# Attention visits in two half steps, five PSUM banks for scores and two for projections, in a two-block forward pass

## The chip, the cores and the metric

The kernel is one program on one core of a Trainium2 chip. A core has TensorE (matmuls, written into PSUM), VectorE, ScalarE and GpSimd (elementwise work) and SyncE, which issues most of the DMAs here. Each runs its own list of instructions in order, and they wait for one another on semaphores. PSUM has eight banks of 128 x 512 fp32. The metric is the device time of one launch in microseconds; several runs are made and the median is compared.

## The reference

Two model blocks follow one another on x of 512 tokens by 1024 channels in fp32. The first block, in which the change lies, is:

```python
h = rms_norm(x, norm_gain, RMS_EPS)
(qa, ka, va, ga, qb, kb, vb, gb, qc, kc, vc, fc, gc, gm) = split(h @ w_in)
ya = diff_attention(qa, ka, va, lam, slopes_a)           # A: 4 heads, each two softmaxes over 64 channels, p0 - lam*p1
ya = rms_norm(ya, subln_gain, SUBLN_EPS) * (1 - lam_init)
yb = sliding_window_attention(qb, kb, vb, sinks, slopes_b)  # B: 8 heads, window of 128
yc = forgetting_attention(qc, kc, vc, log_sigmoid(fc + b_forget))  # C: 8 heads, decay by a cumulative sum
ua, ub, uc = (ya*silu(ga)) @ w_up_a, (yb*silu(gb)) @ w_up_b, (yc*silu(gc)) @ w_up_c
gates = sigmoid(gm)                                      # three gates of 1024
x = x + (gates0*ua + gates1*ub + gates2*uc) @ w_o
```

The attentions are causal over blocks of 128 queries. The second block (a gated recurrence, a linear attention, a short convolution, a convolutional FFN of 2816 channels, an embedding gate) comes afterwards and is not changed.

## The kernel before

**Tiles.** Activations lie with channels on the partitions and the 512 tokens on the free axis. A projection tile is 128 output channels by 512 tokens, one PSUM bank, summed over eight blocks k of 128 input channels. Each k takes three matmuls, for both operands are split into a high part in the fp32r format and the rest: high by high (L911), high by low (L912), low by high (L914). So a tile is 24 matmuls of 128x512. Weights come in units of four blocks (half a tile): SyncE loads a unit into `raw`, ScalarE makes `whi` (L1247), GpSimd makes `wlo = raw - whi` (L2191). There are 5 `raw` and 6 `whi` and `wlo` buffers; a unit is split five units ahead of its use (`LOOK`), and the load of unit u+5 waits on SyncE until `wlo` of unit u is done.

**The order of the work.** `Plan` writes one list of steps, and every engine's program follows that list in order (`follow`), taking from each step what is its own. A step placed between two others therefore stands between them in every engine's queue. `take(ring, tile)` gives a tile a bank, the one of its ring that was taken longest ago, and TensorE waits (`free`) until the bank's last holder has been read. The ring "S" is for scores, transposes and small sums; its banks are 4, 5, 6 and bank 3 as well while projections use "first3" (0, 1, 2). During the value projection vA, which needs four banks at once ("main", 0 to 3), "S" is 4, 5, 6.

**Attention visits.** Attention runs between projection tiles. `pipeline(groups)` is a generator that yields after each visit; `step` advances it, and `slot(i)`, called after each k of a projection tile, calls `step` after k = 7. vA calls it after every second k. Each attention has 16 groups (C and B: a pair of heads for one query block; A: one head for one query block, with two softmaxes). A visit takes two groups, i and i+1. Groups 4t, 4t+1 have keys 128 and 256 wide and 4t+2, 4t+3 have 384 and 512 (B: never over 256). A visit's steps are, in this order:

1. `normal` of group i-1: VectorE divides the exponentials of the second group of the visit before by their sum;
2. `take` of four banks, then `pair` or `scores`: TensorE computes scores (L1016 for B and C, L1030 for A); VectorE adds the bias, finds the maximum and writes P (L1774), which empties the bank; ScalarE takes the exponential in place with its sum (L1322). For C, VectorE builds the bias first from rows N and a column;
3. `pre` for the next visit: SyncE fetches rows N of a head (L2305, C), VectorE makes a head's bias (A, B);
4. `values` of groups i-4, i-3: TensorE multiplies the transposed P by V (L1065); after a head's last block VectorE copies y, and for A ScalarE squares it;
5. `turn` of groups i-2, i-1: TensorE transposes P (L1041) into a bank of "S", ScalarE copies it to SBUF (L1334). It needs `normal` of that group. C has four such tiles where the groups are wide (their width doesn't fit two to a bank), else two;
6. `normal` of group i;
7. for A, every second visit, `late`: TensorE sums the squares (L1071), ScalarE forms the norm (with loads of a table), VectorE applies it.

P has six buffers; P of a group is written again by the score six further on.

**The projections around it.** Ahead of the first visit are kA0 and kA1; then kA and qA tiles run under C's visits, vA too; kB, vBt, qB under A's; the four gateC tiles under A's last ones; nine `gm` tiles under A's last and B's visits; gateA, gateB afterwards. After a tile its `out`, `gate_out` or `gm_out` copies it out of its bank (ScalarE L1310, L1306, L1373; for qB, kB and the gates VectorE as well). In each queue that step stands behind the visit that was called after the tile's k = 7, and ahead of step 1 of the next visit.

Of the kernel before, what the change touches and what calls it, by code (L numbers as in the profile page):

```python
# [132 lines left out]
class Plan:  # L133
# [21 lines left out]
    def add(self, *step):  # L155
        self.steps.append(step)

    def take(self, ring, tile):
        banks = {"main": (0, 1, 2, 3), "first3": (0, 1, 2), "S": (), "Y": (7,), "m3": (0, 1, 2), "x5": (3, 4, 5, 6, 7),
                 "x4": (3, 4), "all": (0, 1, 2, 3, 4, 5, 6, 7)}[ring]  # L160
        if ring == "S":
            banks = self.score_banks
        if ring in ("S", "main", "first3"):
            self.hold(min(banks, key=lambda b: self.held.get(b, -1)), tile)
            return
        n = self.turn.get(ring, 0)
        self.turn[ring] = n + 1
        self.hold(banks[n % len(banks)], tile)
# [29 lines left out]
        self.advance(self.background)  # L198

    def slot(self, i):  # L200
        if i == 7:
            self.step()

    @staticmethod
# [14 lines left out]

    def pipeline(self, groups):  # L220

        n, kind = len(groups), groups[0][0][0]
        for g in groups[0:2]:
            for u in g:
                self.add("pre", *u)
        for i in range(0, n + 6, 2):
            two = groups[i:i + 2]
            if 0 < i <= n:
                for u in groups[i - 1]:
                    self.add("normal", *u)  # L230
            for g in two:
                for u in g:
                    for m in range(2 if kind == "A" else 1):
                        self.take("S", ("scores", *u, m))
                if kind != "A":
                    self.add("pair", *g)
                for u in g:
                    self.add("scores", *u)
            for g in groups[i + 2:i + 4]:
                for u in g:  # L240
                    self.add("pre", *u)
            for g in groups[i - 4:i - 2] if i >= 4 else ():
                _, h, j = g[-1]
                y = ("y" + kind, h if kind == "A" else h // 2 if kind == "C" else h % 4)
                if j == 0:
                    self.take("Y", y)
                self.add("values", kind, h, j)
                if j == 3 and kind != "A":
                    self.ready.add(y)
            for g in groups[i - 2:i] if i >= 2 else ():  # L250
                self.turns(g)
            if two:
                for u in two[0]:
                    self.add("normal", *u)
            if kind == "A" and i >= 6 and groups[i - 5][0][2] == 3:
                h = groups[i - 5][0][1]
                self.take("S", ("late", h))
                self.add("late", h)
                self.ready.add(("yA", h))
            yield  # L260

    def turns(self, units):

        kind, _, j = units[0]
        wd = P * (min(j, 1) + 1) if kind == "B" else P * (j + 1)
        together = [units] if len(units) * wd <= T else [[u] for u in units]
        for us in together:
            slot = self.slots % (4 if kind == "C" else 3)
            self.slots += 1
            for n, u in enumerate(us):  # L270
                self.slot_of[u] = slot, n * wd
            self.slot_before[us[0]] = self.slot_user.get(slot)
            self.slot_user[slot] = us[-1]
            self.take("S", ("turn", *us[0]))
            self.add("turn", *us)

    def stages(self):
        add, take = self.add, self.take
        self.ready = set()
        add("begin")  # L280
        for k in range(KD):
            add("first", k)
            if k <= LOOK:
                self.split_to(k)
        add("lambda")
        for m in range(4):
            take("main", ("kC", m))
        for k in range(KD):
            self.enter("win", k, KC)
            add("kC", k)  # L290
        take("S", ("norm1",))
        add("norm1")
        for m in range(4):
            add("kC_out", m)
        self.tile("S", ("qC", 0))
        take("S", ("columns1",))
        add("columns1")
        add("out", "qC", 0)
        self.tile("S", ("qC", 1))
        add("out", "qC", 1)  # L300
        for m in range(4):
            take("main", ("vC", m))
        take("Y", ("vF", 0))
        for m in range(1, 4):
            take("S", ("vF", m))
        for k in range(KD):
            self.enter("win", k, VC)
            add("vC", k)
            add("x_norm", k)
        add("fc")  # L310
        for half in range(2):
            for m in range(4):
                add("vC_out", half, m)

        def sums(i):
            if i == 5:
                take("S", ("sums",))
                add("sums")

        self.tile("main", ("qC", 2), between=sums)  # L320
        add("out", "qC", 2)
        self.tile("main", ("qC", 3))
        add("out", "qC", 3)
        take("S", ("cq",))
        add("cq")
        c, a, b = softmax_units()
        self.background.append(self.pipeline(c))
        add("masks")
        self.score_banks = (4, 5, 6, 3)
        for name in ("kA", "qA"):  # L330
            for t in range(4):
                self.tile("first3", (name, t), between=None if (name, t) == ("kA", 0) else self.slot)
                add("out", name, t)
        self.score_banks = (4, 5, 6)
        for m in range(4):
            take("main", ("vA", m))
        for k in range(KD):
            self.enter("win", k, VA)
            add("vA", k)
            if k % 2:  # L340
                self.step()
        for m in range(4):
            add("vA_out", m)
        self.background.append(self.pipeline(a))
        self.score_banks = (4, 5, 6, 3)
        for name in ("kB", "vBt"):
            self.tile("first3", (name, 0), between=self.slot)
            add("out", name, 0)
        for t in range(4):
            self.tile("first3", ("qB", t), between=self.slot)  # L350
            add("out", "qB", t)
            if t == 0:
                take("S", ("vB",))
                add("vB")
        self.background.append(self.pipeline(b))

        def gate(name, y, t):
            while (y, t) not in self.ready:
                self.step()
            self.tile("first3", (name, t), between=self.slot)  # L360
            add("gate_out", name, t)

        def gm(d, j):
            take("first3" if self.background else "main", ("gm", d, j))
            self.proj(("gm", d, j), "win", GM + 1024 * j + P * d, between=self.slot)
            add("gm_out", d, j)

        for t in range(4):
            gate("gateC", "yC", t)
        add("masks_in")  # L370
        for d in range(3):
            for j in range(3):
                gm(d, j)
        for t in range(4):
            gate("gateA", "yA", t)
        for t in range(4):
            gate("gateB", "yB", t)
        while self.background:
            self.step()
        add("rg_const")  # L380
        for d in range(8):
            if d >= 3:
                for j in range(3):
                    gm(d, j)
            for n in "cab":
                take("main", ("up", n, d))
                self.proj(("up", n, d), "up_" + n, P * d, range(4))
                add("up_out", n, d)
            add("merged", d)
        add("x_again")  # L390
        for d in range(2):
            take("main", ("wo", d))
            self.proj(("wo", d), "wo", P * d, range(7), stop=False)
        for d in range(8):
            if d < 2:
                self.proj(("wo", d), "wo", P * d, [7], start=False)
            else:
                take("main", ("wo", d))
                self.proj(("wo", d), "wo", P * d)
            add("wo_out", d)  # L400
        self.second(add, take)
# [2045 lines left out]
```

## Time and profile before

| | us |
|---|---|
| median of 3 runs | 1276.0 (1275.64, 1276.0, 1281.35) |
| the profiled execution | 1279.9 |
| its span in the profile | 1278.1 |
| TensorE busy | 1234.3 (97%) |
| VectorE busy | 658.9 (52%) |
| ScalarE busy | 550.4 (43%) |
| GpSimd busy | 659.0 (52%) |
| TensorE's mean granted clock | 0.987 |

The profile comes from one execution. Its span runs from the first instruction to the last; the execution took 1.8 us more. PE is TensorE's matmuls, PEld its weight loads (they overlap the matmuls), DVE VectorE, ACT ScalarE, POOL GpSimd, SP SyncE. Matmuls are pipelined: two of 128x512 start 0.23 us apart although each row shows one as 0.39 long. PEclk is the clock that TensorE was granted as a share of full speed: 1.00 is 2.4 GHz and 0.50 is 1.2 GHz.

### The profile page before, as it was taken

The page shows a single profiled execution, that of the slowest core. Times are in us where ns is not written, and L with a number is a line of the kernel's source. Part 1 is how long each engine was busy: PE and PEld are TensorE (multiplying, and loading weights), DVE is VectorE, ACT ScalarE, POOL GpSimd, SP SyncE. Part 2 cuts the span into 40 slices and gives each one's busy share as a digit, 9 for nine tenths or more (in the row PEclk, how much of TensorE's full clock was granted, in tenths as well). Part 3 has the DMA queues.
Part 4 walks back from the last instruction along what each step waited for, and adds up shares of the span by engine and source line. Part 5 has one row for each costly group of instructions (what it writes and reads, how often), then busy time and mean ns, then how long its engine had stood idle before and what let it go on. Part 6 is the DMA issues. An engine that isn't in the chain of part 4 may idle for free.

```text
span 1278.1 us, 17097 instructions
## 1 busy us (share of the span) xinstructions
PE 1234.3 (97%) x6230; PEld 982.5 (77%) x6230; DVE 658.9 (52%) x1217; ACT 550.4 (43%) x1066; POOL 659.0 (52%) x501
## 2 busy tenths in 40 slices
PE   7998989999999999999989999999999999999996
PEld 5886767777878888888776676878888888888885
DVE  6436744765743312125277545459999999200024
ACT  4544544676654333235552647542332333322344
POOL 4772223235346544446454464646767776655542
PEclk9998999999999999999988999999999999999998
DMA  5333222113222433343231121423333333433321
GB/s 197 112 113 98 67 61 73 50 50 83 67 66 83 114 92 91 95 152 112 82 84 50 42 71 53 116 82 84 99 99 99 90 92 87 128 96 94 100 74 66
DMA packets 63939, 113.94 MB, mean 89 GB/s; under 512 B 7016, under 2 KB 12776, under 8 KB 63856
## 3 DMA queue, kind: packets, MB, share of 16 engines
q1 hardware_dynamic: 63712, 112.84, 31.0%
q8 instruction: 50, 0.82, 0.3%
q14 instruction: 33, 0.27, 0.1%
q10 hardware_dynamic: 144, 0.00, 0.0%
HBM read 110.71 MB, written 2.11 MB: 88 GB/s over the span
## 4 chain that ended last, share of the span: by engine, by line
PE 83%; DVE 9%; ACT 3%; issue 2%; POOL 1%; DMA 1%; DVEq 0%; SPq 0%; ACTq 0%; POOLq 0%
PE pb L911 24%; PE pb L912 24%; PE pb L914 24%; PE pb L1065 2%; PE pb L1041 1%; DVE P L1774 1%; PE pb L1016 1%; POOL HL L2191 1%; DVE B L1644 1%; PE pb L979 1%; DVE U L1644 1%; DVE sq L1632 1%; PE pb L981 1%; PE pb L980 1%; POOL wlo L2191 1%
## 5 line engine op out<-in xcount | busy, mean ns | idle before, releaser
L2191 POOL TENSOR_TENSOR wlo<-raw,whi 128x512 fp32r<-128x512 f32 (+3 forms) x398 | 539.6, 1372 | 437.7 <-ACT whi L1247 437.5
L911 PE MATMUL pb<-HH,whi 128*128 128x512 f32 x968 | 391.4, 404 | 0.0
L912 PE MATMUL pb<-HL,whi 128*128 128x512 f32 x968 | 384.1, 397 | 0.0
L914 PE MATMUL pb<-HH,wlo 128*128 128x512 f32 x968 | 382.6, 395 | 0.0
L1247 ACT ACTIVATE whi<-raw 128x512 fp32r<-128x512 f32 (+3 forms) x398 | 233.2, 613 | 184.5 <-PE pb L914 156.5
L911 PEld LDWEIGHTS pb<-HH,whi 128*128 128x128 f32 x968 | 183.3, 189 | 47.0 <-issue 3.7
L914 PEld LDWEIGHTS pb<-HH,wlo 128*128 128x128 f32 x968 | 182.7, 189 | 42.6
L912 PEld LDWEIGHTS pb<-HL,whi 128*128 128x128 f32 x968 | 182.9, 189 | 42.2 <-issue 2.4
L1644 DVE SCALAR_TENSOR_TENSOR cv<-zf,vecs,cv 128x512 f32<-128x512 f32 x88 | 124.9, 1419 | 3.1
L1322 ACT ACTIVATE P<-P,stat 128x256 f32<-128x256 f32 (+3 forms) x96 | 51.1, 533 | 92.9 <-DVE stat L1639 68.9
L1635 DVE TENSOR_TENSOR X<-pb,X 128x512 f32<-128x512 f32 x24 | 16.6, 691 | 137.7 <-PE pb L914 137.3
L1774 DVE CUSTOM_DVE_ANT_0 P<-pb,B 128x256 f32<-128x256 f32 (+3 forms) x96 | 43.6, 454 | 54.9 <-PE pb L1016 32.9
L1644 DVE SCALAR_TENSOR_TENSOR gms<-gms,pb 128x512 f32<-128x512 f32 x24 | 16.4, 687 | 105.3 <-PE pb L914 105.3
L914 PE MATMUL pb<-fh,wlo 128*128 128x512 f32 x176 | 69.6, 395 | 0.0
L912 PE MATMUL pb<-fl,whi 128*128 128x512 f32 x176 | 69.5, 395 | 0.0
L911 PE MATMUL pb<-fh,whi 128*128 128x512 f32 x176 | 69.3, 394 | 0.0
L2191 POOL TENSOR_TENSOR fl<-cv,fh 128x512 fp32r<-128x512 f32 x22 | 32.3, 1469 | 63.5 <-ACT fh L1574 63.5
L1574 ACT ACTIVATE fh<-cv 128x512 fp32r<-128x512 f32 x22 | 13.9, 632 | 103.6 <-DVE cv L1644 103.6
L1644 DVE SCALAR_TENSOR_TENSOR cv<-cv,cv 128x512 f32<-128x512 f32 x44 | 35.5, 808 | 17.8 <-ACT cv L1569 15.4
L1569 ACT ACTIVATE cv<-cv 128x512 f32<-128x512 f32 x22 | 13.9, 632 | 67.6 <-DVE cv L1644 67.6
L1041 PE MATMUL pb<-cst,P 128*128 128x128 f32 x176 | 28.2, 289 | 12.1 <-DVE stat L1774 11.0
L914 PEld LDWEIGHTS pb<-fh,wlo 128*128 128x128 f32 x176 | 33.0, 188 | 8.1 <-POOL wlo L2191 0.5
(386 smaller groups left out, 1913.1 us busy)
## 6 DMA issues: line engine op xcount, KB each, us to landing
raw<-in_wall SPq DMA_DIRECT2D x362, 256.0 KB, 2.7
raw<-in_wall SPq DMA_DIRECT2D x16, 192.0 KB, 2.4
raw<-in_wall SPq DMA_DIRECT2D x8, 260.0 KB, 3.1
X<-in_xT SPq DMA_DIRECT2D x8, 256.0 KB, 5.3
N<-c_sums SPq DMA_DIRECT2D x8, 256.0 KB, 4.1
X<-in_xT SPq DMA_DIRECT2D x2, 1024.0 KB, 7.7
outT<-PP SPq DMA_DIRECT2D x8, 256.0 KB, 2.2
raw<-in_wall SPq DMA_DIRECT2D x12, 128.0 KB, 2.1
```

The source lines that it names most:

```text
L911: pe.do.matmul(b, hi, xh[k], start=start, stop=False)
L912: pe.do.matmul(b, hi, xl[k], start=False, stop=False)
L914: m = pe.do.matmul(b, lo, xh[k], start=False, stop=stop)
L1041: z = pe.do.transpose(ps(*tile)[:, o + P * j:o + P * j + P], p[:, P * j:P * j + P], ident)
L1065: z = pe.do.matmul(o, w, pt, start=j == 0, stop=j == n - 1)
L1247: a.do.activation(whi[u % NS][:, 0:n], raw[u % NR][:, 0:n], ACT.Copy).then_inc(*up("whi", ("whi", u)))
L1322: a.do.activation(p, p, ACT.Exp, bias=stat(u, 4 * m + 1), accum_out=stat(u, 4 * m + 2)).then_inc(*up("a_exp", ("exp", u, m)))
L1569: a.do.activation(cv[(3 * j + 1) % 6], cv[3 * j % 6], ACT.Tanh, scale=0.5).then_inc(*up("a_gate", ("ffn_tanh", j)))
L1635: v.do.tensor_tensor(dst, x, y, ALU.add).then_inc(*up(name, *points))
L1644: v.do.scalar_tensor_tensor(out=dst, in0=x, scalar=s, in1=y, op0=op0, op1=op1).then_inc(*up(name, *points))
L1774: v.do.tensor_tensor_reduce(Pr[s % 6][:, 0:wd], ps("scores", *u, m)[:, 0:wd], bias, 1.0, LOWEST, ALU.add, ALU.max, stat(u, 4 * m)).then_in ...
L2191: g.do.tensor_tensor(lo, x, hi.bitcast(F32), ALU.subtract).then_inc(*up(name, point))
```

## The change

Four things are changed, all in `Plan`:

- The visit is cut in two. The generator yields after `late` (step 7), and a second half step holds `normal` of the second group (formerly step 1 of the next visit) and `pre` for the next visit (formerly step 3). Visits without a second group, the last three of each pipeline, have no second half step. `slot` steps after k = 3 and after k = 7, and vA after every k.
- The ring "first3" becomes "first2" (banks 0 and 1), and "S" has banks 4, 5, 6, 3 and 2 outside vA. "first2" is used wherever "first3" was, for gateA and gateB too, which run without visits beside them.
- kA0 and kA1 have no slots. The first half step of C comes after k = 3 of kA2; it came after k = 7 of kA1.
- During vA "S" stays at 4, 5, 6.

```diff
     def take(self, ring, tile):
-        banks = {"main": (0, 1, 2, 3), "first3": (0, 1, 2), ...
+        banks = {"main": (0, 1, 2, 3), "first2": (0, 1), ...
...
     def slot(self, i):
-        if i == 7:
+        if i in (3, 7):
             self.step()
...
         for i in range(0, n + 6, 2):
             two = groups[i:i + 2]
-            if 0 < i <= n:
-                for u in groups[i - 1]:
-                    self.add("normal", *u)
             for g in two:
...
                 for u in g:
                     self.add("scores", *u)
-            for g in groups[i + 2:i + 4]:
-                for u in g:
-                    self.add("pre", *u)
             for g in groups[i - 4:i - 2] if i >= 4 else ():
...
             for g in groups[i - 2:i] if i >= 2 else ():
                 self.turns(g)
-            if two:
-                for u in two[0]:
-                    self.add("normal", *u)
+            for u in two[0] if two else ():
+                self.add("normal", *u)
             if kind == "A" and i >= 6 and groups[i - 5][0][2] == 3:
...
             yield
+            if two:
+                for u in two[1]:
+                    self.add("normal", *u)
+                for g in groups[i + 2:i + 4]:
+                    for u in g:
+                        self.add("pre", *u)
+                yield
...
-        self.score_banks = (4, 5, 6, 3)
+        self.score_banks = (4, 5, 6, 3, 2)
         for name in ("kA", "qA"):
             for t in range(4):
-                self.tile("first3", (name, t), between=None if (name, t) == ("kA", 0) else self.slot)
+                self.tile("first2", (name, t), between=None if name == "kA" and t < 2 else self.slot)
...
             add("vA", k)
-            if k % 2:
-                self.step()
+            self.step()
...
-        self.score_banks = (4, 5, 6, 3)
+        self.score_banks = (4, 5, 6, 3, 2)
...
-            self.tile("first3", (name, t), between=self.slot)
+            self.tile("first2", (name, t), between=self.slot)
             add("gate_out", name, t)
```

## Rows read from the trace of the kernel before

**Rows 1.** The page's table of busy time: share of the span and instructions.
```profile
PE 1234.3 (97%) x6230; PEld 982.5 (77%) x6230; DVE 658.9 (52%) x1217; ACT 550.4 (43%) x1066; POOL 659.0 (52%) x501
```
**Rows 2.** Stretches of the span: length, busy PE, PEld, DVE, ACT, POOL, clock, DMA.
```profile
97.00:200.00 103.00, 92.55 (x587) 71.55 (x586) 58.61 (x221) 48.41 (x120) 26.30 (x21) 0.97 0.26 75
200.00:290.00 90.00, 86.32 (x437) 64.58 (x436) 59.21 (x182) 55.70 (x128) 29.57 (x23) 1.00 0.19 53
290.00:350.00 60.00, 59.57 (x376) 46.97 (x375) 39.21 (x163) 38.15 (x115) 24.68 (x19) 1.00 0.28 77
110.00:115.00 5.00, 4.32 (x12) 3.56 (x13) 4.69 (x19) 2.65 (x8) 0.00 (x0) 0.50 0.27 81
```
**Rows 3.** TensorE's waits: us in total, times, longest.
```profile
PE pb L1041 <- DVE stat L1774: 11.0, 17, 3.0
...
PE pb L1016 <- DVE stat L1774: 1.3, 2, 0.9
PE pb L1041 <- DVE P L1644: 1.1, 1, 1.1
...
PE pb L979 <- ACT qA L1310: 1.0, 1, 1.0
```
**Rows 4.** Timeline of TensorE, C visit 4: start, duration, instructions, idle before.
```profile
141.09 0.55 PE L1041 MATMUL pb<-cst,P 128*128 128x128 f32 x3 [0.21 <-DVE stat L1774]
142.20 0.66 PE L1041 MATMUL pb<-cst,P 128*128 128x128 f32 x4 [0.57 <-DVE stat L1774]
143.31 0.66 PE L1041 MATMUL pb<-cst,P 128*128 128x128 f32 x4 [0.46 <-DVE stat L1774]
```
**Rows 5.** Timeline of VectorE, the third read of C visit 4.
```profile
141.71 0.42 DVE L1774 CUSTOM_DVE_ANT_0 P<-pb,B 128x256 f32<-128x256 f32 x1
```
**Rows 6.** Timeline of TensorE, C visit 0 and both transposes of visit 1.
```profile
97.24 0.33 PE L1016 MATMUL pb<-kCh,qCh 64*128 64x128 f32 x2
...
109.12 0.69 PE L1041 MATMUL pb<-cst,P 128*128 128x128 f32 x2 [3.00 <-DVE stat L1774]
110.68 1.12 PE L1041 MATMUL pb<-cst,P 128*128 128x128 f32 x4 [0.87 <-DVE stat L1774]
```
**Rows 7.** Timeline of SyncE's queue, the first rows N.
```profile
97.19 1.78 SPq L2305 DMA_DIRECT2D N<-c_sums  x4
```
**Rows 8.** Timeline of GpSimd, the last weight unit ahead of them.
```profile
95.41 1.31 POOL L2191 TENSOR_TENSOR wlo<-raw,whi 128x512 fp32r<-128x512 f32 x1 [1.04 <-ACT whi L1247]
```
**Rows 9.** Timeline of VectorE, its first instruction of C visit 0.
```profile
101.32 0.35 DVE L1644 SCALAR_TENSOR_TENSOR B<-N,CQ,cst 128x128 f32<-128x128 f32 x1 [15.12 <-DMA N<-c_sums]
```
**Rows 10.** Timeline of TensorE, the transposes of A visit 4.
```profile
239.72 1.05 PE L1041 MATMUL pb<-cst,P 128*128 128x128 f32 x7 [0.96 <-DVE stat L1774]
```
**Rows 11.** Timeline of VectorE, a `normal` of A at two places.
```profile
216.41 0.55 DVE L1641 TENSOR_SCALAR P<-P,stat,sm 128x512 f32<-128x512 f32 x1
...
236.41 1.36 DVE L1641 TENSOR_SCALAR P<-P,stat,sm 128x512 f32<-128x512 f32 x1
```
**Rows 12.** Timeline of GpSimd beside the second of these.
```profile
236.18 2.73 POOL L2191 TENSOR_TENSOR wlo<-raw,whi 128x512 fp32r<-128x512 f32 x2 [8.18 <-ACT whi L1247]
```
**Rows 13.** Timeline of VectorE, the `normal` ahead of A visit 8's second transpose.
```profile
277.33 1.81 DVE L1644 SCALAR_TENSOR_TENSOR P<-P,stat,P 128x512 f32<-128x512 f32 x1
```
**Rows 14.** Timeline of ScalarE, copies after C visits 4 and 5.
```profile
143.99 1.82 ACT L1334 ACTIVATE PT<-pb 128x384 f32<-128x384 f32 x4
...
157.06 0.60 ACT L1310 ACTIVATE qA<-pb 128x512 f32<-128x512 f32 x1
```
**Rows 15.** Timeline of TensorE, the projection's restart after C visit 5.
```profile
153.23 0.47 PE L911 MATMUL pb<-HH,whi 128*128 128x512 f32 x1
```
**Rows 16.** Timeline of TensorE in B: a visit's start, the start two tiles on.
```profile
331.11 0.33 PE L1016 MATMUL pb<-kBh,qBh 64*128 64x128 f32 x2
...
341.95 0.47 PE L911 MATMUL pb<-HH,whi 128*128 128x512 f32 x1
```
**Rows 17.** Timeline of ScalarE, the tanh of the tile ahead of that visit.
```profile
336.56 0.58 ACT L1373 ACTIVATE gms<-pb 128x512 f32<-128x512 f32 x1
```

More of the change, by code:

```diff
@@ L158, in take @@
     def take(self, ring, tile):
-        banks = {"main": (0, 1, 2, 3), "first3": (0, 1, 2), "S": (), "Y": (7,), "m3": (0, 1, 2), "x5": (3, 4, 5, 6, 7),
+        banks = {"main": (0, 1, 2, 3), "first2": (0, 1), "S": (), "Y": (7,), "m3": (0, 1, 2), "x5": (3, 4, 5, 6, 7),
                  "x4": (3, 4), "all": (0, 1, 2, 3, 4, 5, 6, 7)}[ring]
@@ L162, in take @@
             banks = self.score_banks
-        if ring in ("S", "main", "first3"):
+        if ring in ("S", "main", "first2"):
             self.hold(min(banks, key=lambda b: self.held.get(b, -1)), tile)
@@ L344, in stages @@
         self.background.append(self.pipeline(a))
-        self.score_banks = (4, 5, 6, 3)
+        self.score_banks = (4, 5, 6, 3, 2)
         for name in ("kB", "vBt"):
-            self.tile("first3", (name, 0), between=self.slot)
+            self.tile("first2", (name, 0), between=self.slot)
             add("out", name, 0)
         for t in range(4):
-            self.tile("first3", ("qB", t), between=self.slot)
+            self.tile("first2", ("qB", t), between=self.slot)
             add("out", "qB", t)
@@ L359, in gate @@
                 self.step()
-            self.tile("first3", (name, t), between=self.slot)
+            self.tile("first2", (name, t), between=self.slot)
             add("gate_out", name, t)
         def gm(d, j):
-            take("first3" if self.background else "main", ("gm", d, j))
+            take("first2" if self.background else "main", ("gm", d, j))
             self.proj(("gm", d, j), "win", GM + 1024 * j + P * d, between=self.slot)
```

## The prediction

> **What bounds the kernel now.** I read the busy table first: TensorE is busy 1234.3 us, 97% of a span of 1278.1 [rows 1]. Time can only come out of its idle 43.8 us. The change touches the stage in which attention visits run between projection tiles, about 97 to 350 us. The table of stretches [rows 2] puts 10.45 us of idle into 97 to 200 (attention C), 3.68 into 200 to 290 (A) and 0.43 into 290 to 350 (B): 14.6 us in all. What comes after isn't touched, nor is the number of TensorE's instructions.
>
> The list of TensorE's waits [rows 3] says what these are. 11.0 us, 17 times, are a transpose (`turn`, L1041) that waits for L1774, VectorE's read of a score bank; 1.3 us are scores waiting for the same; 1.1 us are one transpose waiting for a `normal`; 1.0 us is vA waiting for qA3's copy out of its bank. Sum 14.4. So mostly it isn't the softmax that is late: a visit takes all four banks for its own scores, and its first transpose needs a bank whose scores were issued a moment ago. Only the 1.1 us is a `normal`.
>
> I number the visits of each attention from 0; "narrow" visits have keys 128 and 256 wide, "wide" ones 384 and 512.
>
> **The fifth bank.** With four banks transpose k of a visit waits until VectorE has read score k; with five it waits for score k-1, and the first for nothing of this visit. Reads in a narrow C visit are 1.11 us apart: that is the spacing of the starts 142.20 and 143.31 [rows 4].
> - C visits 2 and 4 (four transposes; visit 4's waits [rows 4] stand for those of 2 and 6). In visit 4 the waits are 0.21 + 0.57 + 0.46 = 1.24; the last transpose starts at 143.31, and would start when the third read (141.71 + 0.42, and 0.1 to release [rows 5]) is done, about 142.25. That saves 1.06; visit 2, with 0.87 of waits, about 0.75. Sum 1.8, bounds 0 and 2.1.
> - C visit 1. Its transposes wait 3.00 and 0.87 and its scores 0.46. The cause lies one visit back: VectorE could not start on visit 0 (TensorE at 97.24) before the N rows landed at 101.32 [rows 6, 9]. With five banks the first transpose goes early, and the second starts where the first does now, 109.12 instead of 110.68 [rows 6]: 1.56 saved. But moving the first visit doesn't bring N forward. N is queued on SyncE behind a weight load that waits for GpSimd's `wlo`; that ended at 96.72 and N was issued at 97.19, with visit 0 [rows 7, 8]. Half a tile later one more weight block stands ahead of it: it is free at 97.2 when kA1 ends, then copy out (0.6), `whi` (0.6), `wlo` (1.3), load (0.4), so N is issued at about 100.5 against a visit 0 at 97.24 + 2.8 = 100.0. VectorE gets 0.6 us less. Net 0.95; bounds -0.6 and 4.3.
> - A: visits 4 and 6 wait 0.96 and 0.89 [rows 10] for the first. Now both transposes of the visit come after the wait; afterwards only the second does, so the first's 0.35 us and some lateness go: 0.65 each, 1.3 together, bounds 0 and 1.85. The small waits of A and B, four of the 17, are what is left of the 11.0 once those of C visits 1, 2, 4, 6 and 7 and of these two are out: 11.0 - 3.87 - 0.87 - 1.24 - 1.26 - 0.89 - 1.85 = 1.0. They go.
>
> Those 0.96 us rest on a VectorE that is late: its `normal` took 1.36 us for 128x512 at 236.41, while GpSimd ran `wlo` from 236.18, against 0.55 with GpSimd idle [rows 11, 12]. The later step doesn't part them: ScalarE makes the next `whi` right after the exponentials, so `wlo` starts about where `normal` does. I leave this lateness in.
> The Trainium skill, SBUF — State Buffer, section "Who interferes with whom", says that a VectorE instruction with two SBUF inputs or in a two-port mode and a GpSimd one exclude each other for the whole instruction; the trace agrees (1.36 against 0.55). By that rule A's two waits stay and only the moved transposes are won (0.7 in place of 1.3).
>
> **The half tile.** The second group's `normal` no longer stands behind the next tile's end and copy out in VectorE's queue. In C nothing is queued there and VectorE does it at once anyway: 0. In A visit 8 the transpose waits 1.10 us for a `normal` that took 1.81 and stood behind gateC1's two gate products [rows 3, 13]; it will be done before them: 1.1, bounds 0 and 1.1. `pre` moves too: N for the later heads leaves SyncE half a tile later, behind a load whose `whi` is behind the visit's exponentials, some 11 us after the visit and 4 us to land; its reader comes two visits (20 us) on. Cost 0, and up to 3 us if it is late once. TensorE is interrupted as often as now, since the second half has no instruction of TensorE.
>
> **Fewer tiles.** A pipeline has 8 full visits (two half steps each) and 3 without a second group (one half step): 19 half steps, where 11 tiles were. C starts half a tile later and now has six visits, not seven, ahead of vA. vA leaves only three score banks. So the narrow C visit 6 moves into vA. There its fourth score waits for the first read (0.4), and its fourth transpose for ScalarE's copy of the first (ScalarE's four copies start at 143.99 and take 1.82, 0.46 each, so 144.45; the last transpose starts at 143.31 now) [rows 4, 14]. Visit 6 gets 0.65 longer. Visit 7 keeps its waits (0.88 and 0.89), since it already ran in vA. vA's second tile needs qA3's bank: ScalarE copied qA2 out by 157.7 and has one `whi` (0.6) more ahead of it, so 5.1 us after TensorE left visit 5 (153.23), while TensorE needs it after half a tile and 0.7, that is 3.5 [rows 14, 15]. It waits 1.65 instead of 1.00. Sum of both: +1.3, bounds -2.3 (all goes) and +4 (the waits get longer and the clock falls).
> The ends of the pipelines come half a tile after the visit before. `values` need the copies of the transposes (0.9 to 1.9 us in ScalarE) and `late` a copy and a square (0.7 + 0.6); half a tile is 2.8 us: 0, bounds 0 and 2.
>
> **Two projection banks.** A tile's bank is wanted again when the next tile and its visit are through. In B, the tightest place since visits come at the tile's end, the tile was full when the visit began at 331.11, ScalarE's tanh left its bank at 336.56 + 0.58 = 337.1, and the tile after next begins at 341.95 [rows 16, 17]. 4.8 us are left over. In C and A the copy comes 5.1 us after the visit against 2.8 + 5.6. Cost 0, upper bound in the second rival.
>
> **Sum.** 0.95 + 1.8 - 1.3 (C) + 1.3 + 1.1 (A) + 1.0 (the four small ones) = 4.9 us. The profiled execution took 1279.9 (span 1278.1 and 1.8 around it), 3.9 above the median 1276.0 and inside the runs' spread (1275.64 to 1281.35). It would take 1275.0, and the median goes to 1271.1.
>
> **Rivals.**
> - *The stalls nearly all go, and the clock stays up.* After C visit 1's stall the granted clock was 0.50, the lower level of 1.2 GHz, over 110 to 115 with TensorE busy 4.32 us [rows 2]: half of that, 2.2, is lost. If the stall, cut in two by the early transpose, no longer brings the clock down, and VectorE is on time in A, it is 4.9 + 2.2 + 0.55 (A) + 1.3 (vA no worse) = 9.0: 1267. For it: the idle piece gets shorter. Against: 2.7 of 3.0 us stay in one piece.
> The Trainium skill, TensorE: Matmul & The Clock Gate, Part 1, says that the clock falls to half after idleness and returns once the engine is kept busy; the trace agrees with both, and a stall that stays keeps this loss.
> - *Two banks are too few: slower.* The next tile but one waits for a copy out that is queued on ScalarE behind the exponentials. It decides once ScalarE is 4.8 us later than now in B, or 3.3 in the rest. Then about 25 tiles run under visits; at 0.5 us each 12.5 - 4.9 = +7.6: 1283.6. For it: vA already waits 1.0 for just such a copy. Against: the room above.
> - *It doesn't do what it says.* The extra stalls in vA (up to 4) and a late N eat C's gain, and A's stay with the slow `normal`: 1.1 + 1.0 + 0.7 - 1.3 = 1.5: 1274.5.
>
> **How the numbers follow.** Forecast 0.40, its own range 1269 to 1274; all-go rival 0.30; not what it says 0.17; slower rival 0.13. About 0.5% (6.4 us) is what a measurement of this kernel can tell from no change, so faster means under 1269.6: the rival's 0.30 less a few, and 0.04 of the forecast, 0.32. Slower means over 1282.4: 0.11. Between them 0.57. The range 1264 to 1280 leaves out the larger part of the slower rival and a case in which visit 7's waits go as well.
>
> **What would show it.** L1041's wait for L1774 falls from 11.0 to 5 or 6 us and C visits 2 and 4 have nearly none; C visit 1 keeps one idle piece of over 2.5 us and the clock falls after it; in vA there is a wait of 1.5 us or more for a copy out and more idle in visit 6 than now; the 1.10 us on `normal` is gone; no wait of a projection matmul (L911) for a bank in B. I am wrong if L911 waits repeatedly, or if idle in 97 to 350 falls below 6 us.

## The result and the profile after

The changed kernel took 1282.83 us (median of 13 runs, 1279.51 to 1286.3), the kernel before, run beside it, 1279.33 (13 runs, 1274.87 to 1281.51). The ratio is 1.0032, with a 95% interval of 1.0018 to 1.0045: slower by 0.3%, 4 us, where 4.9 us less was forecast. (The kernel before ran 3.3 us over the three runs that the prediction started from, so what is compared is the difference between the two kernels, not the forecast time.) The profiled execution took 1283.07 with a span of 1281.3, 3.2 more than before's 1278.1.

The page's table of busy time answers to [rows 1]. TensorE's work is the same, so the 3.2 us are idle time:

```profile
PE 1234.4 (96%) x6230; PEld 983.8 (77%) x6230; DVE 663.7 (52%) x1217; ACT 549.9 (43%) x1066; POOL 658.7 (51%) x501
```

The table of stretches, columns as in [rows 2]; the third is a part of the first, the fifth and sixth are parts of the fourth (290 to 350):

```profile
97.00:200.00 103.00, 92.84 (x587) 72.02 (x586) 60.28 (x221) 48.16 (x120) 26.71 (x21) 0.97 0.27 75
200.00:290.00 90.00, 88.53 (x459) 66.83 (x458) 62.21 (x184) 57.10 (x130) 30.48 (x23) 1.00 0.20 56
110.00:115.00 5.00, 2.12 (x7) 1.91 (x8) 4.83 (x14) 1.46 (x5) 1.81 (x2) 0.67 0.58 161
290.00:350.00 60.00, 54.06 (x356) 42.90 (x356) 43.61 (x183) 37.37 (x120) 20.70 (x16) 0.94 0.23 61
295.00:300.00 5.00, 0.89 (x5) 0.90 (x5) 4.62 (x15) 2.44 (x7) 2.71 (x2) 0.60 0.00 0
300.00:303.00 3.00, 3.00 (x10) 2.38 (x9) 2.82 (x11) 3.00 (x13) 2.62 (x3) 0.53 0.18 34
```

Idle in C went from 10.45 to 10.16 us, in A from 3.68 to 1.47, and in B from 0.43 to 5.94. Attention B, to which the prediction gave no cost, has 5.5 us more of idle, and the clock fell with it: 0.94 over the whole stretch, where it was 1.00. TensorE's waits (total, times, longest) name the reason in the first row, which answers to the 11.0 us of [rows 3]:

```profile
PE pb L1041 <- DVE stat L1774: 13.4, 9, 5.4
...
PE pb L1016 <- DVE stat L1774: 1.5, 2, 0.9
...
PE pb L979 <- ACT qA L1310: 1.3, 1, 1.3
```

Nine waits where there were 17: most of the small ones went, as forecast, but one of 5.4 us is new. The wait on `normal` (L1644) is gone.

TensorE's timeline round it, attention B's visits 0 and 1 (visit 0's scores at 284.92, the two units of visit 1 at 291.55, then the transposes):

```profile
281.17 1.02 PE L1071 MATMUL pb<-W,cst 128*128 128x512 f32 x2
...
284.92 0.33 PE L1016 MATMUL pb<-kBh,qBh 64*128 64x128 f32 x2
...
291.55 0.39 PE L1016 MATMUL pb<-kBh,qBh 64*128 64x256 f32 x2
...
299.11 1.11 PE L1041 MATMUL pb<-cst,P 128*128 128x128 f32 x4 [5.36 <-DVE stat L1774]
```

VectorE in that time, where the transpose's releaser is the read at 298.63:

```profile
287.82 0.75 DVE L1644 SCALAR_TENSOR_TENSOR qA<-qA,sm,W 128x512 f32<-128x512 f32 x1 [3.89 <-ACT W L1263]
288.49 1.60 DVE L1639 TENSOR_SCALAR B<-cst 128x256 f32<-128x256 f32 x2
290.01 0.28 DVE L1774 CUSTOM_DVE_ANT_0 P<-pb,B 128x128 f32<-128x128 f32 x1
...
293.07 0.29 DVE L1639 TENSOR_SCALAR P<-P,stat 128x128 f32<-128x128 f32 x1
295.14 0.69 DVE L1644 SCALAR_TENSOR_TENSOR th<-th,pb 128x512 f32<-128x512 f32 x1 [1.78 <-ACT th L1363]
...
297.51 1.20 DVE L1639 TENSOR_SCALAR P<-P,stat 128x256 f32<-128x256 f32 x1
298.63 0.41 DVE L1774 CUSTOM_DVE_ANT_0 P<-pb,B 128x256 f32<-128x256 f32 x1
```

And ScalarE, for which VectorE waited twice:

```profile
285.14 1.28 ACT L1236 ACT_TABLE_LOAD   x1
286.43 0.69 ACT L1259 ACTIVATE W<-pb,sm 128x512 f32<-128x512 f32 x1
287.16 0.63 ACT L1263 ACTIVATE W<-W 128x512 f32<-128x512 f32 x1
...
293.21 1.28 ACT L1363 ACT_TABLE_LOAD   x1
294.51 0.60 ACT L1363 ACTIVATE th<-pb 128x512 f32<-128x512 f32 x1
```

Read together: the last head of A is normalised by `late(3)`, whose sum TensorE makes at 281.17. ScalarE needs another table for its logarithm, and VectorE's product with it, at 287.82, stands ahead of everything of attention B. Visit 0's scores have waited since 284.92 and are read at 290.01, 5.1 us late. Then the gate's tanh needs the other table again, VectorE waits 1.78 us for it, and the gate's two products (from 295.14) stand between visit 0's two groups. Visit 1's scores, issued at 291.55, are read at 298.63. Before, visit 0's scores came at 299.80, 6.5 us after `late(3)`'s matmul (293.26); now they come 3.75 us after it.

### The profile page after: what moved, and what is told of

Its sections match the earlier page's. It is cut to its first block, busy times and chain, and to the rows that moved or that the text cites. A ratio compares the mean times of both kernels' runs of the same rounds, so it can differ in the third digit from the quotient of the medians.

```text
span 1281.3 us, 17102 instructions
## 1 busy us (share of the span) xinstructions
PE 1234.4 (96%) x6230; PEld 983.8 (77%) x6230; DVE 663.7 (52%) x1217; ACT 549.9 (43%) x1066; POOL 658.7 (51%) x501
## 4 chain that ended last, share of the span: by engine, by line
PE 80%; DVE 10%; ACT 4%; issue 3%; POOL 1%; DMA 1%; DVEq 0%; SPq 0%; ACTq 0%; POOLq 0%
PE pb L911 24%; PE pb L912 24%; PE pb L914 23%; PE pb L1065 1%; PE pb L1041 1%; DVE P L1774 1%; PE pb L1016 1%; ACT L1236 1%; POOL HL L2191 1%; PE pb L979 1%; DVE U L1644 1%; PE pb L981 1%; PE pb L980 1%; DVE sq L1632 1%; POOL wlo L2191 1%
## 5 line engine op out<-in xcount | busy, mean ns | idle before, releaser
L911 PE MATMUL pb<-HH,whi 128*128 128x512 f32 x968 | 392.4, 405 | 0.0
L911 PEld LDWEIGHTS pb<-HH,whi 128*128 128x128 f32 x968 | 183.7, 190 | 47.1 <-issue 3.6
L1644 DVE SCALAR_TENSOR_TENSOR cv<-zf,vecs,cv 128x512 f32<-128x512 f32 x88 | 124.8, 1418 | 3.1
L1644 DVE SCALAR_TENSOR_TENSOR gms<-gms,pb 128x512 f32<-128x512 f32 x24 | 16.4, 686 | 105.4 <-PE pb L914 105.4
L911 PE MATMUL pb<-fh,whi 128*128 128x512 f32 x176 | 69.3, 394 | 0.0
L1644 DVE SCALAR_TENSOR_TENSOR cv<-cv,cv 128x512 f32<-128x512 f32 x44 | 35.5, 808 | 17.8 <-ACT cv L1569 15.4
L911 PEld LDWEIGHTS pb<-fh,whi 128*128 128x128 f32 x176 | 33.2, 188 | 7.8
```

The costliest lines, as they stand in the source:

```text
L911: pe.do.matmul(b, hi, xh[k], start=start, stop=False)
L1644: v.do.scalar_tensor_tensor(out=dst, in0=x, scalar=s, in1=y, op0=op0, op1=op1).then_inc(*up(name, *points))
```

## Where the time went, stage by stage

The start of the same projection matmul in the two timelines gives the gap of after to before. Negative is ahead. Where more visits are done in one kernel than in the other, their matmuls are taken out of the last column:

| up to | gap, us | so the stage gave |
|---|---|---|
| the end of qA's tiles (C visits 0 to 5) | -1.77 | -1.77 |
| the end of vA | -0.11 | +1.66 |
| the first `gm` tile (after has already done `late(3)`'s 0.5 us of matmuls and B visit 0's 1.0, before has not) | -1.82 | -3.2 |
| the end of attention (start of gateB3) | +3.67 | +6.9 |

The 6.9 us of B are 5.5 us more of idle (the piece of 5.36 and smaller waits of 0.39 and 0.20, against 0.43 before) and matmuls at the lower clock behind the idle piece (0.53 in 300 to 303): from the end of that visit to the next visit TensorE took 6.8 us, where the same stretch took 5.4 before.

## Experiments

The same gap, at the start of gateB3, is given for each kernel below beside the ratio to the kernel before. From here on it is counted from kA0's first matmul: what a profiled execution was ahead or behind by then, up to 1.2 us, arose ahead of attention and is taken off (0.02 for the changed kernel, so its +3.67 becomes +3.65). The starting theory was that B's visit 0 comes too soon after `late(3)`; the rivals were that five score banks, or the half steps themselves, cost the time.

**e1: attention B enters with the first `gm` tile, half a tile later.**
```diff
-        self.background.append(self.pipeline(b))
...
         for t in range(4):
             gate("gateC", "yC", t)
+        self.background.append(self.pipeline(b))
         add("masks_in")
```

> Attention B starts after the four gateC tiles (first half step after k = 3 of gm 0,0) in place of after k = 7 of gateC 3; all else as in the changed kernel. Theory J (the loss sits where A ends and B begins: VectorE and ScalarE still hold late(3) and the gateC products with their table loads when B's first scores come): the 5.4 us wait of L1041 in 290 to 305 us goes, L1041's wait for L1774 falls from 13.4 to about 8, no clock at 0.5 there, and the time is about 3.5 us under the kernel before (ratio 0.997). Rival P (the two projection banks and five score banks do it, wherever B starts): a wait of over 3 us stays in B's first visits, time 2 to 4 us over before. Rival H (B's second half step is always late): the same.

Measured: ratio 1.0025 [1.0012, 1.0037], gap +3.41: 0.2 us of the gap came back, and 0.07% of the ratio, less than its interval is wide. The miss tells that half a tile is too little, not that the place is right. TensorE's timeline has three idle pieces in place of one:

```profile
296.73 0.30 PE L1041 MATMUL pb<-cst,P 128*128 128x128 f32 x1 [1.33 <-DVE P L1639]
...
299.08 0.33 PE L1041 MATMUL pb<-cst,P 128*128 128x128 f32 x1 [2.05 <-DVE P L1639]
...
300.73 1.11 PE L1041 MATMUL pb<-cst,P 128*128 128x128 f32 x4 [1.32 <-DVE stat L1774]
```

VectorE read visit 0's scores only at 292.06, and a one-column addition then took 1.15 us beside GpSimd's cast of the masks:

```profile
292.06 0.28 DVE L1774 CUSTOM_DVE_ANT_0 P<-pb,B 128x128 f32<-128x128 f32 x1
...
294.15 1.15 DVE L1635 TENSOR_TENSOR stat<-stat 128x1 f32<-128x1 f32 x1
```
```profile
293.71 1.57 POOL L2215 CAST cu<-maskf 128x1664 uint8<-128x1664 f32 x1
295.24 3.71 POOL L2191 TENSOR_TENSOR wlo<-raw,whi 128x512 fp32r<-128x512 f32 x3
```

**e2: the banks alone** (the kernel before with whole visits, five banks for scores, two for projections).
```diff
-        banks = {"main": (0, 1, 2, 3), "first3": (0, 1, 2), ...
+        banks = {"main": (0, 1, 2, 3), "first2": (0, 1), ...
...
-        self.score_banks = (4, 5, 6, 3)
+        self.score_banks = (4, 5, 6, 3, 2)
```

> The kernel before with only the rings changed: five banks for scores and transposes, two for projections; visits whole and after k = 7, first visit after kA1. Theory J: B then begins after gm 0,1 as before, so no stall there; L1041's wait for L1774 falls from 11.0 to about 6, C visits 2, 4 and 6 nearly free of waits, C visit 1 saves 1.5; time 4 to 5 us under before (ratio 0.9965). Rival P: projection matmuls (L911) wait for their bank, or B's first visits stall by over 3 us; time over before.

Measured: 0.9981 [0.9969, 0.9993], gap -2.98. The banks are a gain, and the two-bank rival falls. What they cost is at one place, vA's entry, where the wait of [rows 3] for qA3's bank grew from 1.0:

```profile
164.34 0.73 PE L979 MATMUL pb<-whi,HH 128*128 128x512 f32 x1 [2.80 <-ACT qA L1310]
```

**e3: the half steps alone** (the changed kernel with three and four banks).
```diff
-        banks = {"main": (0, 1, 2, 3), "first2": (0, 1), ...
+        banks = {"main": (0, 1, 2, 3), "first3": (0, 1, 2), ...
...
-        self.score_banks = (4, 5, 6, 3, 2)
+        self.score_banks = (4, 5, 6, 3)
```

> The changed kernel with the old rings: four banks for scores, three for projections; half steps and the later first visit stay. Theory J: the stall at B's second visit stays (over 5 us, clock down after it), C's narrow visits wait as in the kernel before, A visit 8's 1.1 us is gone, vA costs 1 to 2 us more; time 6 to 8 us over before (ratio 1.0055). Rival P: the stall is gone and the time is within 2 us of before.

Measured: 1.006 [1.0041, 1.008], gap +9.52. So the half steps, with the starts that come with them, lose 9 us by themselves: 3.6 by the end of vA, 7.9 in B, with 2.0 won in A between them. In B scores wait 1.45 us and a transpose 4.57. TensorE's waits, first row:

```profile
PE pb L1041 <- DVE stat L1774: 15.7, 15, 4.6
```

**e4: attention C starts a tile sooner** than in the changed kernel, in the middle of the second kA tile (kA1). That is half a tile sooner than in the kernel before.
```diff
-                self.tile("first2", (name, t), between=None if name == "kA" and t < 2 else self.slot)
+                self.tile("first2", (name, t), between=None if name == "kA" and t < 1 else self.slot)
```

> The changed kernel with C's first half step after k = 3 of kA1, a full tile earlier than in the changed kernel (kA0 alone has no slots), so that seven C visits stand ahead of vA, as in the kernel before. The stall at B stays. Theory V (narrow C visit 6 inside vA costs 1.7 us): vA's waits fall, time 1 to 2 us under the changed kernel, so 2 us over before (ratio 1.0015). Rival N (an earlier first visit waits longer for the rows N, whose DMA is held behind weight loads): C visit 1's wait grows by 2 us or more and nothing is won.

Measured: 1.0005 [0.9993, 1.0017], 0.27% under the changed kernel; gap +2.50. The gap at the end of vA went from -0.13 to -1.70. These 1.6 us are a balance. Visit 6, again ahead of vA, takes 4.74 us where it took 6.80 within vA, and vA's entry waits 0.52 where it waited 1.27: 2.8 us won. C visit 1, also a tile sooner, takes 8.46 where it took 7.24, with waits of 0.49, 0.73 and 3.75: 1.2 us lost.

**e5: attention B enters after the first `gm` tile**, in the middle of the second. Before, visit 0 came at that tile's end; in the changed kernel two tiles sooner, at the end of gateC's last.
```diff
-        self.background.append(self.pipeline(b))
...
                 gm(d, j)
+                if d == 0 and j == 0:
+                    self.background.append(self.pipeline(b))
```

> The changed kernel with attention B started after gm 0,0 (first half step after k = 3 of gm 0,1), where the kernel before has it within half a tile. The start one half tile later (e1) left B's stall in place, with VectorE reading B's first scores 4.3 us late behind late(3) and gateC 3, so the junction theory J, in the form that the late norm and the gate products with their table loads (5 us on ScalarE from 285.2 to 290.3) must be over when B starts, expects: no wait over 1 us in B, no clock at 0.5 there, 7 us less than the changed kernel, 3 to 4 us under before (ratio 0.997). Rival H (half steps as such make B's start stall; the place doesn't matter, as e1 suggests): a stall of 3 us or more again, ratio 1.0025.

Measured: 0.9988 [0.9976, 1.0000], gap -3.05: 6.7 us less than the changed kernel at that tile, 0.44% (5.6 us) in the ratio. 0.7 us of the 6.7 were there by the end of vA, where the two kernels are still the same, so 6.0 came with the edit. Nothing else differs (every tile has the same bank in both), so the place of B's first visit is the cause. In its timeline and its stretch (columns as above; its line numbers are one higher) visit 1 waits 1.16 and the clock stays up. One projection matmul now waits for its bank, 0.45 us at 289.51, for the gate's product that reads it; e6 and e11, which start B here too, have the same wait.

```profile
292.51 0.33 PE L1017 MATMUL pb<-kBh,qBh 64*128 64x128 f32 x2
...
301.68 0.66 PE L1042 MATMUL pb<-cst,P 128*128 128x128 f32 x4 [1.16 <-DVE stat L1775]
```
```profile
290.00:350.00 60.00, 58.84 (x384) 46.59 (x384) 43.25 (x179) 37.93 (x122) 24.65 (x19) 1.00 0.26 70
```

**e8: how much of the stall is `late(3)`?** For the last head ScalarE's table load, logarithm and exponential become one copy. That head is then not normalised; only the time is read. The table load of the next tanh goes as well.
```diff
-                tables(LNEXP)
+                if h < 3:
+                    tables(LNEXP)
+                if h == 3:
+                    a.do.activation(Wr[h % 3], ps("late", h), ACT.Copy)...
+                    return
```

> The changed kernel, with the norm of A's last head left out on ScalarE: late(3) is one copy in place of a table load, a logarithm and an exponential, and the table load of the next tanh goes as well (that head of A isn't normalised). Start of B unchanged. Theory J expects VectorE to reach B's first scores some 3 us earlier (1.3 + 0.6 before late's product, 1.3 for gateC 3's tanh), B's stall of 5.4 to fall to 2 or 3 us and the clock to stay up: 3 to 5 us less than the changed kernel (ratio 0.9995). Rival H: the stall stays over 4.5 us, ratio 1.003.

Measured: 1.0017 [1.0004, 1.003], gap +1.99, and the stall is 3.8 (waits in 282 to 360):

```profile
PE pb L1041 <- DVE stat L1779: 3.8, 1, 3.8
```
The product was 2.3 us earlier (285.49), but visit 0's first read only 1.1 (288.89), since the two bias operations ahead of it took 2.68 us beside GpSimd, where they took 1.60.

**e9: how much is the gate between the groups?** B's first visit is made whole, with its second group called ahead of the gate's products.
```diff
             self.tile("first2", (name, t), between=self.slot)
+            if (name, t) == ("gateC", 3):
+                self.step()
             add("gate_out", name, t)
...
-            self.proj(("gm", d, j), ..., between=self.slot)
+            self.proj(("gm", d, j), ..., between=(lambda i: i == 7 and self.step()) if (d, j) == (0, 0) else self.slot)
```

> The changed kernel, with B's first visit kept whole: its second half step (normal of the second group) is called right after its first, ahead of gateC 3's gate_out, and not after k = 3 of gm 0,0; B's second visit stays where it was. Theory J has two parts in the 5.4 us: VectorE reads B's first scores 5 us late (late(3)), and then gate_out of gateC 3 stands for 3.2 us (293.3 to 296.5) between the two normals, so the next scores are read that much later. If the second part counts by the order of the queue alone, that order doesn't shorten the queue: gate_out still precedes the second visit's reads, VectorE only fills its idle 1.8 us (293.4 to 295.1) with the normals, and the stall falls by 1.5 to 2 us, to 3.5 to 4; 1.5 to 2.5 us less than the changed kernel (ratio 1.0015). If it doesn't count, 5.4 us stay and the ratio is 1.003.

Measured: 1.0010 [0.9999, 1.0021], gap +2.42. The stall fell to 3.2:

```profile
PE pb L1043 <- DVE stat L1776: 3.2, 1, 3.2
```
The gate's products still stand ahead of visit 1's reads here. What moved is the second group's `normal`: its 2.2 us (296.47 to 298.63, with the 1.20 above) no longer stand behind them, but in the time in which VectorE waited for the tanh. So `late(3)`'s chain, with the tanh's table load, accounts for 1.6 of the 5.4 us, and the place of that `normal` behind the products for 2.2. The two were not taken away together.

**e7: e2, and vA's tiles handed their banks so that qA3's goes to the last.**
```diff
-        for m in range(4):
-            take("main", ("vA", m))
+        last = self.bank["qA", 3]
+        rest = sorted((b for b in range(4) if b != last), key=lambda b: self.held.get(b, -1))
+        for m, bank in enumerate([*rest, last]):
+            self.hold(bank, ("vA", m))
```

> The kernel before with only the rings changed (as e2), and vA's four banks given out so that the one that qA 3 fills is used by vA's last tile, not its second. In e2 vA waited 2.8 us there for ScalarE's copy (1.0 in the kernel before). Theory W (the rings' gain is eaten at vA's entry): that wait goes or is under 0.5, and the time is 2 to 3 us under e2's, 4.5 to 5.5 under before (ratio 0.996). Rival: the copy is late for the last tile as well, or the wait moves to vA's value banks 2 and 3: time as e2 (ratio 0.998).

Measured: 0.9960 [0.9946, 0.9974], median 1273.59, gap -5.61. The entry of vA now waits for something else, a copy of transposes, and for less (line numbers two higher):

```profile
162.97 0.50 PE L981 MATMUL pb<-whi,HH 128*128 128x512 f32 x1 [1.58 <-ACT PT L1336]
```

**e6: the changed kernel with e4's, e5's and e7's edits together** (half steps, everything put right).

> The changed kernel with three edits: B from gm 0,1 (e5), C's first half step after k = 3 of kA1 (e4, which took 1.5 us off up to vA's end), and vA's banks as in e7. If the terms add: -3.8 (e5) - 1.1 to -1.5 - 0.5 to -1.3, so 5.5 to 6.5 us under before (ratio 0.9955). If B's stall is H's, ratio 1.000 or over.

Measured: 0.9959 [0.9943, 0.9975], median 1272.59, gap -5.69. No different from e7, which has whole visits. C visit 1 still waited 3.8.

**e10: e7, and C's first N rows fetched a tile ahead of visit 0.** **e11: e6 with the same edit**, where it comes half a tile ahead.
```diff
         for g in groups[0:2]:
             for u in g:
                 self.add("pre", *u)
+        if kind == "C":
+            yield
...
                 add("out", name, t)
+                if (name, t) == ("kA", 0):
+                    self.step()
```

> e7 (whole visits, two and five banks, vA's order) with C's first rows N fetched after kA 0, a tile before the first visit. Theory N (C visit 1's stall of 2.8 us, 3.0 in the kernel before, and the fall of the clock after it come from rows N that SyncE issues only with the visit): VectorE begins with TensorE's first scores at 98 and not at 101, visit 1's wait is under 0.5 us, the clock stays at 1.00 over 105 to 115, and the time is 4 us under e7's, 9 to 10 under before (ratio 0.9925). Rival: VectorE's reads at 1.1 us each are the limit in visit 1, N or not; then 1 us or less is won (ratio 0.9955).

> e6 (half steps, two and five banks, B from gm 0,1, C from k = 3 of kA 1, vA's order) with the rows N fetched after kA 0, half a tile before the first visit. Theory N: visit 1's stall of 3.8 us goes, ratio 0.9925 as for e10. If half steps bring nothing once the junction and the rows N are mended, e10 and e11 are equal within 0.1%; if spreading the second group's normal helps, e11 is 1 to 2 us under e10.

Measured: e10 0.9933 [0.9917, 0.9949], median 1270.55, gap -9.42. e11 0.9940 [0.9925, 0.9955], median 1271.06, gap -7.01. In e10 the rows leave SyncE at 93.29, where they left at 97.19 [rows 7]; VectorE starts 3.0 us sooner than in [rows 9]; and visit 1's wait, 3.00 + 0.87 in [rows 6], is 0.49. SyncE, VectorE, TensorE and two stretches of e10 (line numbers six higher):

```profile
93.29 0.83 SPq L2311 DMA_DIRECT2D N<-c_sums  x2
```
```profile
98.33 0.35 DVE L1650 SCALAR_TENSOR_TENSOR B<-N,CQ,cst 128x128 f32<-128x128 f32 x1 [12.22 <-DMA N<-c_sums]
```
```profile
106.16 0.65 PE L1047 MATMUL pb<-cst,P 128*128 128x128 f32 x4 [0.49 <-DVE stat L1780]
```
```profile
97.00:200.00 103.00, 96.84 (x622) 75.40 (x622) 62.79 (x237) 51.27 (x131) 28.48 (x22) 1.00 0.27 80
110.00:115.00 5.00, 4.91 (x41) 3.63 (x39) 4.75 (x16) 3.75 (x11) 1.36 (x2) 1.00 0.00 0
```

Idle in attention C is 6.2 us where it was 10.45, and the stretch that ran at half clock [rows 2] runs at full clock. Visit 2 pays a part back: it waits 0.54 and 0.95, where it waited for nothing in e7. In e11 visit 1 still waited 3.5 us. There the rows leave at the same time, 93.33, but visit 0 comes 2.7 us sooner, so VectorE still starts 3.2 us behind it (1.2 in e10). e10 is the fastest kernel of the case: 0.67% under the one before.

| kernel | visits | banks | ratio | gap, us |
|---|---|---|---|---|
| changed | half steps | 5 + 2 | 1.0032 | +3.65 |
| e3 | half steps | 4 + 3 | 1.006 | +9.52 |
| e5 | half, B later | 5 + 2 | 0.9988 | -3.05 |
| e6 | half, all put right | 5 + 2 | 0.9959 | -5.69 |
| e11 | e6, N early | 5 + 2 | 0.9940 | -7.01 |
| e2 | whole | 5 + 2 | 0.9981 | -2.98 |
| e7 | whole, vA's banks | 5 + 2 | 0.9960 | -5.61 |
| e10 | e7, N early | 5 + 2 | 0.9933 | -9.42 |

## Why the prediction was wrong

The failed step is "Fewer tiles", in its last sentence: "half a tile is 2.8 us: 0, bounds 0 and 2". It asked whether `values` and `late` are in time for their own pipeline. It counted 19 half steps where 11 tiles were, and did not draw the consequence that A's pipeline ends 1.5 tiles sooner and takes the start of B's with it, two tiles sooner, into the one that holds `late(3)`'s table loads and the gate's products. That cost 6.9 us in the profile, and e5 gets 6.0 of them back by that one edit (5.6 us by the ratio). No rival had it: the slower rival was about projection banks, and in the changed kernel no projection matmul (L911) waited for one. e8 took away the late norm's chain and e9 the place of the second `normal` behind the gate's products, and the stall shrank by 1.6 and 2.2 us of 5.4; e1 shows that a move of half a tile only changes what VectorE is late for. The remaining 1.6 us was not tried: the gate's two products (1.4 us) are still ahead of visit 1's reads in both kernels, and two bias operations took 1.60 (288.49) beside GpSimd's work, but that this is the rest is argued.

The other steps, each against its own size:
- C visits 2 and 4: forecast 1.8, came 1.8. Visit 2 took 3.72 us where it took 4.83, visit 4 4.75 where it took 5.41. Visit 4 keeps two waits, 0.24 and 0.46.
- C visit 1: forecast 0.95 net, came 0.1. The chain of the N rows was right: issue worked out at 100.5, seen at 100.39. But the prediction took VectorE's work up to visit 1's first read as unchanged, and it grew by 1.0 us (from the first instruction of visit 0 to that read 8.18, where it was 7.18). Two of its operations now fall beside GpSimd's `wlo`, where it was one. Changed kernel, VectorE, GpSimd and TensorE, then VectorE before:

```profile
109.31 1.38 DVE L1639 TENSOR_SCALAR P<-P,stat 128x256 f32<-128x256 f32 x1
110.61 1.34 DVE L1644 SCALAR_TENSOR_TENSOR B<-N,CQ,cst 128x128 f32<-128x128 f32 x1
...
109.25 2.56 POOL L2191 TENSOR_TENSOR wlo<-raw,whi 128x512 fp32r<-128x512 f32 x2 [9.33 <-ACT whi L1247]
...
112.88 1.12 PE L1041 MATMUL pb<-cst,P 128*128 128x128 f32 x4 [3.75 <-DVE stat L1774]
```
```profile
107.08 1.38 DVE L1639 TENSOR_SCALAR B<-N,CQ 128x256 f32<-128x256 f32 x1
```

  The visit itself became 0.62 us shorter (7.24 for 7.86). The idle piece of 3.75 us took the clock down with it, 0.50 from 112 to 118, and the tile behind took 7.66 us where it took 7.12: 0.5 of the 0.6 went again.
- vA: forecast +1.3, came +1.66. The entry's wait was put at 1.65 and was 1.27; visit 6 was put at 0.65 longer and took 1.37 more, with waits of 0.62, 0.62, 0.62 and 0.54.
- A with the small waits: forecast up to 3.4, came 3.2. Visit 4 still waits 0.51, visit 6 0.97. The `normal` of 1.10 us is gone, as forecast.
- Two projection banks: forecast 0, came 0.

As measured, the terms without B are 1.8 + 3.2 - 1.7 = 3.3 us of gain, where the sum had 4.9, and e5, with B's start moved back, is 3.1 ahead at the end of attention. So the sum was 1.6 us too high where it looked, most of it in C visit 1 (0.9), and the one place that it priced at nothing turned what was left into a loss.

None of the prediction's cases had the larger lesson: the gain is in the banks alone. Whole visits with five banks (e2) beat the change by 0.5%, and once the starts are put right, half steps add nothing (e6 against e7, e11 against e10). With four banks for scores they cost 9 us (e3), 7.9 of it in B, whose start was not put right there; half steps with four banks and the right starts were not run. The 3.6 us that e3 loses by the end of vA are not settled either: its timeline has waits of 3.98 and 0.62 at C visit 1, and visit 6 within vA takes 7.33 us where it took 5.43.

## What to carry to other kernels

When a pipeline that runs in another's gaps gets denser, write down the tile at which each pipeline now ends and the next one starts, and read what the helping engines do at that tile. A start that costs under half a microsecond in one place stalled TensorE for 5.4 us two tiles sooner. A change made of several parts is best run part by part: here one part alone was faster than the whole. And where rings of banks change hands, give the bank whose copy out comes last to the tile that needs it last (2.6 us here, e7 against e2), and fetch the rows of a pipeline's first visit well ahead (3.8 us, e10 against e7).

## What the runs showed of the hardware

A piece of idle time costs TensorE more than its length. After the 5.36 us the clock was 0.53 in 300 to 303, with TensorE busy all the time. After e10's 0.49 and e5's 1.16 it stayed at 1.00. In e7 a piece of 2.76 us stood between:

```profile
109.14 1.11 PE L1043 MATMUL pb<-cst,P 128*128 128x128 f32 x4 [2.76 <-DVE stat L1776]
```

There four transposes took 1.11 us, as after the long stalls, where four take 0.66 elsewhere: the lower level again (0.52 in 110 to 115, with TensorE busy all the time). Three pieces of 1.33, 2.05 and 1.32 with little between them (e1) did the same: the clock was 0.50 in 300 to 305.

VectorE's short operations lose as much beside GpSimd as its long ones: in e1 an addition of one column took 1.15 us instead of 0.15, and in the changed kernel a 128x256 `normal` took 1.38 instead of 0.35. The Trainium skill, SBUF — State Buffer, section "Who interferes with whom", speaks of an exclusive lock held for a whole instruction, not of a shared rate. The trace agrees: the addition ended at 295.30 and GpSimd's cast of 1.57 us at 295.28, so the extra 1.0 us is what was left of the cast, whatever VectorE's own size.
